# A list scheduler's latency table: one wait per pair of engines in place of one per producer

## The reference

```
h = x
for i in range(2):
    u, bg, cg, v = split(rmsnorm(h) @ w_in[i])             # 1024 -> 4 x 512
    y_pool = pool_mixer(u)      # windows of 2, 4, 8, 16 tokens, minus the token, then 128x128 maps
    y_conv = bg * short_conv(cg * v)                       # three taps along the tokens
    h = h + concat(y_pool, y_conv) @ w_out[i]
    f = relu(rmsnorm(h) @ w_up[i])                         # 1024 -> 4096
    h = h + (f * f) @ w_down[i]                            # 4096 -> 1024
    h = h + sigmoid(rmsnorm(h) @ w_gate[i]) * (p[i] @ w_proj[i])
y = rmsnorm(h)
```

## Time and profile before

| | |
|---|---|
| median of 3 runs | 1455.05 us (1454.87 to 1456.32) |
| the profiled execution's own time | 1455.05 us |
| its span, slowest core (core 1) | 1453.4 us (cores: 1450.8 to 1453.4) |
| TensorE busy | 1404.0 us, 97% of the span, 7690 matmuls |
| VectorE busy | 1261.9 us, 87% |
| ScalarE busy | 730.5 us, 50% |
| GpSimd busy | 98.6 us, 7% |
| mean DMA rate | 75 GB/s |

### The profile page before, as it was taken

One profiled execution on the slowest core, in us unless ns is written; L12 is line 12 of the kernel. 1 busy time (PEld: TensorE's weight loads), 2 busy tenths in 40 slices (PEclk: granted clock), 3 DMA queues, 4 the chain that ended last, 5 costly groups with the idle time before them and its releaser, 6 DMA issues.

```text
span 1453.4 us, 25302 instructions; the slowest of 8 cores (1450.8 to 1453.4 us)
## 1 busy us (share of the span) xinstructions
PE 1404.0 (97%) x7690; PEld 664.8 (46%) x7690; DVE 1261.9 (87%) x2630; ACT 730.5 (50%) x1310; POOL 98.6 (7%) x190
## 2 busy tenths in 40 slices
PE   8999999999999999999999999999999999999995
PEld 5544454344444444443544445444344445444444
DVE  5989899888999877799897998888889988779998
ACT  5553355543553633547534442843554553535766
POOL 3000010000000000100000001100000000000000
PEclk9999999999999999999999999999999999999998
DMA  9900097554444444540050006955554444440124
GB/s 206 222 21 1 1 163 113 88 87 74 87 74 73 74 74 73 87 74 14 11 88 1 1 1 94 150 87 75 86 88 73 74 73 71 75 74 1 22 91 166
DMA packets 31637, 109.23 MB, mean 75 GB/s; under 512 B 3440, under 2 KB 6000, under 8 KB 30704
## 3 DMA queue, kind: packets, MB, share of 16 engines
q0 software_dynamic: 26656, 95.30, 39.1%
q1 hardware_dynamic: 4560, 11.52, 2.2%
q10 hardware_dynamic: 288, 0.79, 0.2%
HBM read 185.38 MB, written 10.10 MB: 134 GB/s over the span
## 4 chain that ended last, share of the span: by engine, by line
PE 84%; DVE 8%; issue 4%; ACT 3%; DMA 0%; DVEq 0%; ACTq 0%
PE ps L435 84%; DVE arena L1005 2%; DVE arena L745 1%; ACT sq L726 1%; DVE sq L714 1%; DVE h L1133 1%; DVE h L1118 1%; DVE arena L1115 1%; DMA h<-x_all 0%; ACT L682 0%; ACT arena L1108 0%; DVE arena L923 0%; ACT ps L945 0%; DVE arena L830 0%; DVE ps L977 0%
## 5 line engine op out<-in xcount | busy, mean ns | idle before, releaser
L435 PE MATMUL ps<-arena,ring 128*128 128x512 bf16 (+4 forms) x5296 | 944.1, 329 | 17.7 <-ACT arena L1108 3.8
L435 PEld LDWEIGHTS ps<-arena,ring 128*128 128x128 bf16 (+1 forms) x5296 | 449.7, 98 | 455.8 <-issue 51.1
L435 PE MATMUL ps<-arena 128*128 128x512 f16 (+3 forms) x2144 | 525.3, 376 | 9.4 <-ACT ps L945 5.6
L435 PEld LDWEIGHTS ps<-arena 128*128 128x128 f16 (+1 forms) x2144 | 194.9, 97 | 294.6 <-issue 107.6
L945 ACT ACTIVATE ps<-ps 128x512 f32<-128x512 f32 x256 | 148.9, 582 | 321.2 <-PE ps L435 275.1
L1020 DVE TENSOR_TENSOR h<-h,ps 128x512 f32<-128x512 f32 x384 | 250.8, 684 | 41.8 <-PE ps L435 35.7
L726 ACT ACTIVATE sq<-h 128x512 bf16<-128x512 f32 x223 | 131.3, 623 | 89.1 <-DVE h L1020 31.4
L745 DVE SCALAR_TENSOR_TENSOR arena<-h,vec,rstd 128x512 bf16<-128x512 f32 (+3 forms) x224 | 143.5, 665 | 2.2 <-ACT rstd L684 2.2
L1001 ACT ACTIVATE arena<-ps 128x512 f32<-128x512 f32 x192 | 113.9, 594 | 61.9 <-PE ps L435 47.2
L923 DVE TENSOR_TENSOR arena<-arena 128x512 f16<-128x512 f16 (+1 forms) x288 | 124.8, 452 | 18.9 <-ACT arena L995 13.9
L938 DVE TENSOR_TENSOR arena<-ring 128x512 f16<-128x512 f16 x256 | 106.9, 420 | 7.1 <-PE ps L435 6.6
(11 more groups left out here) (64 smaller groups left out, 747.0 us busy)
## 6 DMA issues: line engine op xcount, KB each, us to landing
ring<-w_up POOLq DMA_DIRECT2D x64, 512.0 KB, 5.7
ring<-w_down POOLq DMA_DIRECT2D x64, 512.0 KB, 5.7
ring<-w_in POOLq DMA_DIRECT2D x16, 512.0 KB, 9.9
y_all<-h SPq DMA_DIRECT2D x6, 1024.0 KB, 5.6
h<-x_all POOLq DMA_DIRECT2D x4, 1024.0 KB, 45.5
ring<-w_out POOLq DMA_DIRECT2D x8, 512.0 KB, 31.1
ring<-w_gate POOLq DMA_DIRECT2D x8, 512.0 KB, 5.8
h<-x_all POOLq DMA_DIRECT2D x6, 512.0 KB, 19.5
```

Source lines behind the costliest of these rows:

```text
L435: return eng.matmul(self.psum[o.ps.bank][:, o.col:o.col + o.width], lhsT=l, rhs=r, start=(o.fresh and j == 0), stop=(o.last and j == n - 1 ...
```

## The change

The two figures are replaced by a table `LAT` by pair (producer's engine, consumer's engine), with 190 ns for pairs not in it. The planner's bookkeeping follows: an operation's `end` is now its real end without the latency, and the latency is added where a consumer looks at it (in the due times, in the ready times, in the time at which a bank is free). A bank that TensorE reopens is free 300 ns after its last reader's end; before, `SEMLAT` was in effect counted twice there, 180 ns.

```
-SEMLAT = 90.0
-PELAT = 190.0
+LAT = {("pe", "act"): 165.0, ("pe", "dve"): 185.0, ("act", "act"): 185.0, ("dve", "dve"): 130.0, ("act", "pe"): 300.0, ("dve", "pe"): 300.0,
+       ("pool", "pe"): 300.0}
+OTHER = 190.0
...
+def lat(d, o):
+    return DMALAT if d.chan is not None else LAT.get((d.eng, o.eng), OTHER)
...
-            a = min([s.alap for s in o.succ], default=o.due)
-            a = min(a, o.cap + o.cost + SEMLAT)
-            lat = DMALAT if o.chan is not None else (PELAT if o.eng == "pe" else SEMLAT)
+            a = min([s.alap - lat(o, s) for s in o.succ], default=o.due - OTHER)
+            a = min(a, o.cap + o.cost)
...
-            a -= dur + lat
+            a -= dur
...
-                r = 0.0 if o.after is None else o.after.end - PELAT
+                r = 0.0 if o.after is None else o.after.end
                 for n, (_, _, ds) in enumerate(o.mms):
                     for d in ds:
-                        r = max(r, vis[d] - n * o.per)
+                        r = max(r, d.end + (lat(d, o) if d.eng != "pe" else 0.0) - n * o.per)
             else:
-                r = max([vis[d] for d in o.deps], default=0.0)
+                r = max([d.end + lat(d, o) for d in o.deps], default=0.0)
...
-        def bank_time(n):
+        def bank_time(n, e):
...
-            return max(r.end for r in p.readers) + SEMLAT
+            return max(r.end + LAT.get((r.eng, e), OTHER) for r in p.readers)
...
-            o.start, o.end = tau, vis[o]
+            o.start, o.end = tau, end
```

More of the change, by code:

```diff
@@ L258, in schedule @@
         first_set = 0
-        vis = {}
         def make_ready(o):
             if o.mms is not None:
-                r = 0.0 if o.after is None else o.after.end - PELAT
+                r = 0.0 if o.after is None else o.after.end
                 for n, (_, _, ds) in enumerate(o.mms):
                     for d in ds:
-                        r = max(r, vis[d] - n * o.per)
+                        r = max(r, d.end + (lat(d, o) if d.eng != "pe" else 0.0) - n * o.per)
             else:
-                r = max([vis[d] for d in o.deps], default=0.0)
+                r = max([d.end + lat(d, o) for d in o.deps], default=0.0)
             ready[o] = r
@@ L297, in schedule @@
                         pe_first += 1
-                    bt = [(bank_time(n), n) for n in range(8)]
+                    bt = [(bank_time(n, e), n) for n in range(8)]
                     bt = [x for x in bt if x[0] is not None]
@@ L314, in schedule @@
                         f = self.fillers[0]
-                        r = max([free[e], bfree] + [vis.get(d, 1e12) for d in f.deps])
+                        r = max([free[e], bfree] + [1e12 if d.end is None else d.end + lat(d, f) for d in f.deps])
                         if r + f.cost < tau:
@@ L362, in schedule @@
                 end = dma_free
-                vis[o] = end + DMALAT
             elif e == "pe":
-                vis[o] = end + PELAT
                 o.prev = None
@@ L375, in schedule @@
                 pe_done[pe_pos[o]] = True
[L376 to L380, removed]
-            o.start, o.end = tau, vis[o]
+            elif o.opens is not None:
+                o.opens.bank, o.prev = bank, banks[bank]
+                banks[bank] = o.opens
+            o.start, o.end = tau, end
             order[e].append(o)
```

## The result

The changed kernel takes 1405.99 us (1405.38 to 1406.92) against 1455.41 in the runs beside it: a ratio of 0.966, 95% interval 0.9644 to 0.9677, 49.4 us faster. I had forecast 1421.6, and 1407 to 1447 as the range; the gain is half as large again as my 33.5 us, and the time lies 1 us outside.

The account below looks back on a forecast made before the run. The prediction took short TensorE waits inside the MLP sets, 41.9 us in all, as the loss; filling 0.8 of them, with zero elsewhere, gave 1455.05 - 33.5 = 1421.6 us, range 1407 to 1447.

Parts of the forecast that it names:

- my 33.5 us: Gain expected in the MLP sets: 0.8 of the 41.9 us that TensorE loses there in waits.
- The loss and its place: In the MLP sets TensorE waits behind copies (line 945) and line 1005: 0.327 us per set; the mixer loses nothing.
- That the planner would see them: With the new table the planner sees waits of 97 ns behind copies and 229 ns behind line 1005, over its 30.
- The substitute: At a wait it sees, the planner starts X of the next set instead, giving 0.86 us of cover.
- four of five cases, fewer where banks are short: How often X of the next set can fill a wait in the MLP sets: a factor of 0.8.
- It stays in force: After one swap in the MLP sets, the next set is that much ahead from then on: 0.86 us of cover.
- the 41.9: Microseconds lost to waits in the 128 MLP sets; the upper bound of the gain there.
- The rest of the span I put at zero: Outside the sets, as at MLP stage ends, VectorE sets the pace, so no gain: zero, with bounds.
- my allowance at 6 either way: Bounds in us on the rest of the span, about three pairs of stage-end waits, as the order there changes too.
- Only part is filled: Rival: copies find a substitute, the 0.30 us behind line 1005 stays in 64 up sets: 1437 us; 20 in 100.
- Nothing moves: Rival: every set keeps its waits because X of the next set finds no bank: 1453 to 1457 us; 8 in 100.
- VectorE's queue takes over: Rival: weight sums put before bank-freeing additions make TensorE wait 0.47 us in each set: 1473 us; 8 in 100.

Follow-up runs that it names:

- e5: The changed kernel with 200 ns in place of 300 from ScalarE and from VectorE to TensorE: 1428.04 us.
- e6: The changed kernel with 240 ns in place of 300 from ScalarE and from VectorE to TensorE: 1407.11 us.
- e9: The changed kernel, but TensorE takes the first group in program order that can start within 150 ns of the earliest, before 30: 1427.4 us.
- e3: The changed kernel with 300 ns from ScalarE to TensorE kept, but 90 ns from VectorE to TensorE: 1425.18 us.
- e4: The changed kernel with 300 ns from VectorE to TensorE kept, but 90 ns from ScalarE to TensorE: 1432.02 us.
- e8: The changed kernel with AHEAD = 0, so no set may start before the one before it has placed its last group: 1510.27 us.
- e16: The changed kernel with ScalarE and VectorE to TensorE back at 90 ns, 180 ns for a bank; other pairs as in the change: 1445.12 us.
- e17: The changed kernel with AHEAD = 2 and WINDOW = 60, before 1 and 40, so two sets may start early: 1400.2 us.
- e18: The changed kernel with 90 ns, as before, between ScalarE and VectorE in both directions: 1409.57 us.

## Why the prediction was right or wrong, point by point

**The loss and its place.** Right. The waits behind line 945 and line 1005 are what the change removes, the mixer stands as it did (372 matmuls start from 84 to 164 us, 371 before), and the count of matmuls per stretch found what the view of the waits hides. The forecast was some 733 wide matmuls in 160 us; 648 in 140 are 741 in 160.

**That the planner would see them.** Right: the threshold behind a copy stands where its sum puts it, between 200 and 240 ns (e5, e6, e9); the one behind line 1004 was not bracketed so closely, it lies between 90 (e3) and 200 (e5). The waits are separate terms in e3, but only in part in e4.

**The substitute.** The mechanism was right (the timeline after, e8), but "four of five cases, fewer where banks are short" was wrong. It is every case: the factor was 1.0 within the sets. The reason fell with it, since six banks do. I had counted the taken banks at one instant of the order before and feared that one free bank in the down sets would not do; the planner has that bank when it needs it. "It stays in force" holds only in part: an early set covered the wait behind the first copy in e4's first half, and not the one behind line 1004 in e3. With the factor at 1.0 the sum had been 41.9 us; measured as the share of the entries to TensorE, it is 39.1. It can be read by place, too, from the first and last start of the bank copies of each layer on core 1, before (line 945) and after (line 944):

```profile
L945 ACT ACTIVATE ps<-ps x128: 548/582/599, 201.4 to 642.4; 128x512 f32<-128x512 f32 x128
L945 ACT ACTIVATE ps<-ps x128: 546/582/601, 906.6 to 1348.9; 128x512 f32<-128x512 f32 x128
L944 ACT ACTIVATE ps<-ps x128: 575/582/610, 199.7 to 620.0; 128x512 f32<-128x512 f32 x128
L944 ACT ACTIVATE ps<-ps x128: 573/582/606, 879.8 to 1299.8; 128x512 f32<-128x512 f32 x128
```

The two MLPs went from 441.0 and 442.3 us to 420.3 and 420.0, together 43.0 shorter, of 50.0 us by which the span of this core shrank (1453.4 to 1403.4). So the term of 33.5 was mis-sized by its factor of 0.8; the 41.9 that it was taken of comes close to the 43.0.

**"The rest of the span I put at zero".** This is the other half of the error. By place, 7.0 us were won outside the two MLPs, with my allowance at 6 either way; by entries, those that don't lead to TensorE gave 10.3 us on their own (e16), some of it inside the MLPs (439.5 and 438.7 us long there). I read a busy VectorE as a stage that no order can shorten; in the gating stage of layer 0 waits of 2.8 us became 1.2 by order alone (e16), and e17 shows the same at 407 us, where the change itself had won next to nothing. 39.1 and 10.3 make the 49.4, as 43.0 and 7.0 make the 50.0 of the core.

**The rivals.** *Only part is filled* would have left the waits at line 1005; e3 shows that order, but only with 90 ns from VectorE to TensorE. *Nothing moves* rested on banks. The rule of the Trainium skill that the prediction cites there (Perfetto Trace Analysis, Optimization Strategy) says only that repeating gaps can mean too little SBUF or PSUM for the next tile. Here they did not mean too few banks: the regular gaps went with the same eight, and stay away with six. *VectorE's queue takes over*: VectorE is busy 89% of the span and idles 15.5 us in 140 (124.47 busy); no new wait of that kind stands in the sets.

**Left open.** Which of the other entries gives what outside the sets: e18 takes two of them back for 3.6 us, and the rest of the 10.3 has no run of its own.

## What to carry to other kernels

A static order is only as good as the latencies behind it: where a planner believes a trip to be 0.2 us shorter than it is, it leaves the same small wait in every round and sees none. Add up the believed trip (there, the work, and back), compare it with the trace and with the work put in between; what counts is on which side of that work the sum falls, not its last 50 ns. On a pipelined engine count the instructions of a stretch against their spacing, since waits shorter than the listed duration don't show as idle; and don't price the ends of stages at nothing because one engine is busy there.
